# One transpose of raw queries taken off TensorE, and four small interruptions of a projection joined into two

## The reference

```python
h = rms_norm(x, pre_norm_w)
proj = h @ w_in                         # 4096 x 15408, columns: qa, za, ga, kc, vc, ksl, vsl, kw, vw, qb, kb, vb, zb
gates = sigmoid(ga + b_gate)            # 3 gates for each of 16 heads
kc, vc = compress(kc, ...), compress(vc, ...)     # gelu(blocks @ w1) @ w2: 15 compressed keys and values for each kv head
sc = q_raw @ kc.T                       # raw (not rotated) queries against compressed keys
p_cmp = softmax(where(valid, sc, NEG))
q_rot = rope(q, pos)                    # rotated queries, for the selected and the window branch
o = gates0 * (p_cmp @ vc) + gates1 * o_slc + gates2 * o_win
mix = concat([o * silu(za), ob * silu(zb)])
out = x + rms_norm(mix @ w_out, post_norm_w)
```

## Time and profile before

| what | value |
|---|---|
| median of 3 runs | 1765.64 us (1765.54 to 1766.12) |
| profiled execution: its own time | 1765.85 us |
| profiled execution: span | 1763.9 us |
| TensorE busy | 1757.8 us (100% of the span), 7902 matmuls |
| VectorE busy | 1153.4 us (65%) |
| ScalarE busy | 886.8 us (50%) |
| GpSimd busy | 598.9 us (34%) |
| granted TensorE clock | full in all 40 slices |
| bytes moved by DMA | 344.77 MB, mean 195 GB/s |

### The profile page before, as it was taken

The page is one execution under the profiler, slowest core; times in us unless marked ns, Lnnn a source line. Parts: engine busy times, 40 slices in busy tenths (PEclk is TensorE's granted clock), DMA queues, the critical chain, the costliest instruction groups (busy, mean ns, idle before and its releaser), DMA issues.

```text
span 1763.9 us, 22877 instructions
## 1 busy us (share of the span) xinstructions
PE 1757.8 (100%) x7902; PEld 1456.4 (83%) x7902; DVE 1153.4 (65%) x1192; ACT 886.8 (50%) x1216; POOL 598.9 (34%) x834
## 2 busy tenths in 40 slices
PE   9999999999999999999999999999999999999998
PEld 7888888888888888888888888888888888888886
DVE  7657656787888878656665666566655784444445
ACT  7643455464554545456435643564456554444443
POOL 3335303367593948721353034304431510000000
PEclk9999999999999999999999999999999999999999
DMA  9866687656565656666666666666666656667665
GB/s 294 254 199 188 188 248 229 179 161 185 157 189 151 185 160 174 183 197 182 179 195 196 182 181 197 194 190 176 191 194 191 190 185 217 213 213 212 213 202 204
DMA packets 184267, 344.77 MB, mean 195 GB/s; under 512 B 15216, under 2 KB 19568, under 8 KB 184176
## 3 DMA queue, kind: packets, MB, share of 16 engines
q1 hardware_dynamic: 183456, 342.58, 66.2%
q10 hardware_dynamic: 720, 0.93, 0.1%
HBM read 339.27 MB, written 4.19 MB: 195 GB/s over the span
## 4 chain that ended last, share of the span: by engine, by line
PE 99%; DMA 0%; ACT 0%; SPq 0%; DVE 0%; ACTq 0%; issue 0%
PE acc L640 31%; PE acc L646 31%; PE acc L643 31%; PE acc L821 1%; PE scores L810 0%; PE scores L709 0%; DMA raw<-in_w_in 0%; PE scores L742 0%; PE scores L741 0%; PE scores L740 0%; PE heads L757 0%; PE heads L758 0%; PE heads L759 0%; PE scores L665 0%; PE heads L692 0%; PE trans L657 0%
## 5 line engine op out<-in xcount | busy, mean ns | idle before, releaser
L1239 DVE TENSOR_TENSOR w_parts<-raw,w_parts 128x1024 fp32r<-128x1024 f32 x620 | 784.4, 1266 | 556.9 <-ACT w_parts L929 555.3
L929 ACT ACTIVATE w_parts<-raw 128x1024 fp32r<-128x1024 f32 x620 | 656.2, 1059 | 662.6 <-PE acc L646 649.6
L640 PE MATMUL acc<-w_parts,x_parts 128*128 128x512 f32 x2424 | 946.7, 391 | 0.2 <-DVE w_parts L1239 0.2
L646 PE MATMUL acc<-w_parts,x_parts 128*128 128x512 f32 x2424 | 943.8, 389 | 0.0
L643 PE MATMUL acc<-w_parts,x_parts 128*128 128x512 f32 x2424 | 943.3, 389 | 0.0
L646 PEld LDWEIGHTS acc<-w_parts,x_parts 128*128 128x128 f32 x2424 | 455.1, 188 | 95.8 <-DVE x_parts L1281 0.3
L640 PEld LDWEIGHTS acc<-w_parts,x_parts 128*128 128x128 f32 x2424 | 455.3, 188 | 93.4 <-issue 0.6
L643 PEld LDWEIGHTS acc<-w_parts,x_parts 128*128 128x128 f32 x2424 | 455.3, 188 | 93.0
L515 POOL COPY rot<-tok_b 32x256 f32<-32x256 f32 x120 | 86.9, 724 | 140.6 <-DVE tok_b L1613 135.7
L499 POOL TENSOR_TENSOR rot<-tok_a,trig 128x512 f32<-128x512 f32 x18 | 30.6, 1699 | 260.5 <-ACT tok_a L935 121.4
L515 POOL COPY b_first_t<-probs 32x128 f32<-32x128 f32 x64 | 31.1, 485 | 163.1 <-DVE probs L1686 160.6
(11 more groups left out here) (240 smaller groups left out, 1010.1 us busy)
## 6 DMA issues: line engine op xcount, KB each, us to landing
raw<-in_w_in SPq DMA_DIRECT2D x478, 512.0 KB, 3.7
raw<-in_w_out SPq DMA_DIRECT2D x128, 512.0 KB, 4.3
raw<-in_w SPq DMA_DIRECT2D x16, 512.0 KB, 4.7
x_tok<-in_x SPq DMA_DIRECT2D x16, 256.0 KB, 5.3
xt_raw<-in_x_t SPq DMA_DIRECT2D x7, 512.0 KB, 6.2
wpost<-in_post_w SPq DMA_DIRECT2D x8, 256.0 KB, 5.1
out<-y SPq DMA_DIRECT2D x3, 512.0 KB, 2.8
out<-y SPq DMA_DIRECT2D x5, 256.0 KB, 2.1
```

Of the source, the lines that this page charges most:

```text
L640: nc.tensor.matmul(o, stat_hi, mov_hi, start=(k == 0), stop=False)
L646: last = nc.tensor.matmul(o, stat_lo, mov_hi, start=False, stop=(k == KB - 1))
L929: nc.scalar.activation(w_hi[:, n % SPLIT_SLOTS, :, 0:width], raw[:, n % RAW_SLOTS, :, 0:width], ACT.Copy).then_inc(hi_ready, 1)
L1239: V.tensor_tensor(w_lo[:, s, :, 0:width], raw[:, n % RAW_SLOTS, :, 0:width], w_hi[:, s, :, 0:width].bitcast(F32), ALU.subtract).then_inc(l ...
```

## The change

Tile 1 of each group's raw queries is turned by VectorE (one transpose of 32x32 blocks of 128x512, in place in `tok_a`, at `at` 0, ahead of the split of pair 3), and the 16 blocks are moved to `qraw_t` by GpSimd (rows 0 and 1 of blocks: eight copies of 32x128) and by ScalarE (row 2 at `at` 1 and row 3 at `at` 2: four copies each, the first four ahead of `take_fill` of tile 0). TensorE's second `transpose4` and ScalarE's second `take_fill` go. TensorE waits for both movers ahead of pair 3. GpSimd does its copies ahead of the rotation of tile 0. In chunk `C_QA0` the gates' products follow the hidden layer's ahead of pair 2, and the compressed keys' stand with the values' ahead of pair 9; gates and keys are written to the bank `scores` in place of `trans`. ScalarE takes the keys at `at` 9 in place of 7.

```diff
@@ -70,7 +70,7 @@
 FILL_TRIG, FILL_HIDDEN, FILL_GATE, FILL_KC, FILL_VC, FILL_A = 0, 1, 2, 3, 4, 5
-FILLS_A = 2
+FILLS_A = 1
 TILES_ROTATED = 4
@@ -313,6 +313,9 @@
         heads_taken = sem("heads_taken")
+        q_turned = sem("q_turned")
+        q_moved_pool = sem("q_moved_pool")
+        q_moved_act = sem("q_moved_act")
         q_cos_ready = sem("q_cos_ready")
@@ -538,15 +541,24 @@
             nc.gpsimd.memset(pc_t[:, :, :, :, :].bitcast(F32), 0.0).then_inc(pc_zeroed, 1)
+            pool.wait_ge(pc_zeroed, 1)
             pool.wait_ge(tr_free, FILL_TRIG + 1)
             def rotate_a(g):
+                pool.wait_ge(q_turned, g + 1)
+                move_blocks(tok_a[:, 1:2, :].rearrange("p t (h d) -> p t h d", h=HPG),
+                            qraw_t[:, :, P:SEQ].rearrange("p h (t q) -> p t h q", t=1),
+                            range(QUARTERS * QUARTERS // 2)).then_inc(q_moved_pool, 1)
+                pool.wait_ge(q_moved_pool, g + 1)
                 for t in range(TILES):
...
                     cos = turn_t[:, 1, cols].unsqueeze(1).broadcast_to([P, HPG, P])
-                    pool.wait_ge(tr_free, FILL_A + t + 1 + FILLS_A * g)
+                    if t == 0:
+                        pool.wait_ge(tr_free, FILL_A + 1 + FILLS_A * g)
+                    else:
+                        pool.wait_ge(q_moved_act, g + 1)
                     nc.gpsimd.tensor_tensor(turned, qraw_t[:, :, cols], cos, ALU.mult).then_inc(q_cos_ready, 1)
@@ -696,12 +708,13 @@
-                if n in (1, 2):
-                    t = n - 1
-                    pe.wait_ge(acc0_free if t == 0 else acc1_free, c)
-                    transpose4(tok_a[:, t, :], fill + t)
+                if n == 1:
+                    pe.wait_ge(acc0_free, c)
+                    transpose4(tok_a[:, 0, :], fill)
                 if n == 3:
-                    pe.wait_ge(tr_free, fill + 2)
+                    pe.wait_ge(tr_free, fill + 1)
+                    pe.wait_ge(q_moved_pool, g + 1)
+                    pe.wait_ge(q_moved_act, g + 1)
@@ -835,27 +848,23 @@
                     last.then_inc(tr_done, 1)
-                if n == 3:
                     pe.wait_ge(gate_moved, 2)
-                    pe.wait_ge(tr_free, FILL_GATE)
                     for t in range(TILES):
                         for j in range(2):
-                            last = nc.tensor.matmul(trans[:, t * N_GATE:(t + 1) * N_GATE],
+                            last = nc.tensor.matmul(scores[:, t * N_GATE:(t + 1) * N_GATE],
                                                     gate_sum[:, t * P:(t + 1) * P],
...
                     last.then_inc(tr_done, 1)
-                if n == 7:
+                if n == 9:
                     pe.wait_ge(gelu_ready, 1)
...
                     for j in range(2):
-                        last = nc.tensor.matmul(trans[:, 0:64], w2_sb[:, 0, j, :], gelu[:, j * P:j * P + 64],
+                        last = nc.tensor.matmul(scores[:, 0:64], w2_sb[:, 0, j, :], gelu[:, j * P:j * P + 64],
                                                 start=(j == 0), stop=(j == 1))
                     last.then_inc(tr_done, 1)
-                if n == 9:
                     pe.wait_ge(rows_ready, 1)
-                    pe.wait_ge(tr_free, FILL_VC)
                     for g in range(GROUPS):
@@ -1028,8 +1037,8 @@
                                          ).then_inc(tanh_done, 1)
-                if at == 7:
-                    take_fill(FILL_KC, kc_t[:, :], trans[:, 0:64], 0.5)
+                if at == 9:
+                    take_fill(FILL_KC, kc_t[:, :], scores[:, 0:64], 0.5)
                 if at == 12:
@@ -1057,18 +1066,25 @@
-            def move_quarters(src, dst, rows, cols):
+            def move_quarters(src, dst, rows, cols, t=slice(0, TILES)):
                 rows, cols = slice(rows * QUARTER, (rows + 1) * QUARTER), slice(cols * QUARTER, (cols + 1) * QUARTER)
-                return nc.scalar.activation(dst[cols, :, :].rearrange("p h (t q) -> p t h q", t=TILES)[:, :, :, rows],
-                                            src[rows, :, :].rearrange("p t (h d) -> p t h d", h=HPG)[:, :, :, cols],
+                return nc.scalar.activation(dst[cols, :, :].rearrange("p h (t q) -> p t h q", t=TILES)[:, t, :, rows],
+                                            src[rows, :, :].rearrange("p t (h d) -> p t h d", h=HPG)[:, t, :, cols],
                                             ACT.Copy)
...
                     if at in (1, 2):
-                        take_fill(fill + at - 1, qraw_t[:, :, (at - 1) * P:at * P])
+                        if at == 1:
+                            act.wait_ge(q_turned, g + 1)
+                        for cols in range(QUARTERS):
+                            last = move_quarters(tok_a, qraw_t, at + 1, cols, slice(1, 2))
+                        if at == 1:
+                            take_fill(fill, qraw_t[:, :, 0:P])
+                        else:
+                            last.then_inc(q_moved_act, 1)
                     if at in (4, 5):
@@ -1419,7 +1435,7 @@
                         last = V.scalar_tensor_tensor(gates[:, t, :, :].rearrange("p h b -> p (h b)"),
-                                                      trans[:, t * N_GATE:(t + 1) * N_GATE], r[t], b_gate,
+                                                      scores[:, t * N_GATE:(t + 1) * N_GATE], r[t], b_gate,
                                                       ALU.mult, ALU.add)
@@ -1504,8 +1520,11 @@
             def crossed_halves(t, g, fill):
-                dve.wait_ge(tr_free, fill + t + 1)
-                if t == 1:
+                if t == 0:
+                    dve.wait_ge(tr_free, fill + 1)
+                else:
+                    dve.wait_ge(q_moved_pool, g + 1)
+                    dve.wait_ge(q_moved_act, g + 1)
                     dve.wait_ge(q_rot_ready, 1 + 2 * g)
@@ -1522,6 +1541,9 @@
                     at = n - LEAD
+                    if at == 0:
+                        dve.wait_ge(acc1_free, c)
+                        V.transpose(tok_a[:, 1, :], tok_a[:, 1, :]).then_inc(q_turned, 1)
                     if at in (2, 3):
```

## The result

The changed kernel takes 1770.43 us (median of 11 runs, 1770.12 to 1770.70) against 1765.97 us (11 runs, 1765.54 to 1766.62): ratio 1.0024, 95% interval 1.0016 to 1.0033. It is slower by 4.46 us, 0.25%, where 2 us less were forecast, and lies outside the forecast range of 1762.8 to 1767.0. The profiled execution has a span of 1768.3 us.

What follows compares the result with a forecast made beforehand. TensorE alone was taken to bound the kernel. Its terms, 1.96 + 0.08 = 2.04 us less, gave 1763.6 us against a median of 1765.64, called "same"; range 1762.8 to 1767.0.

Steps and rivals of the forecast that it cites:

- What bounds the kernel: Whole run: TensorE alone carries the chain, its longest wait 1.2 us, so nothing another engine does costs time now.
- The gain: TensorE, four groups: one interruption with four transposes fewer in each, 0.49 us apiece, 1.96 us less.
- the joining: TensorE's small products of gates and compressed keys: two interruptions fewer at 0.04 us each save 0.08 us.
- rival 2: Interruptions on TensorE cost more, so joining saves up to 0.98 us: 2.94 us less, 1762.7 us; chance 0.05.
- TensorE's new wait: Scores with compressed keys, 446.37 in group 1, wait for ScalarE's and GpSimd's copies; 0.4 to 1.9 us spare, no wait.
- Behind it ... Cost 0: After GpSimd's copies: tile 0's cosine product up to 2 us later, 2.5 us spare at pair 6, cost 0.
- The absorption: VectorE's second sine product stood behind the split of pair 5 anyway (448.2), which absorbs most of the delay.
- VectorE's part: Added transpose, 0.70 us a group, ahead of the split of pair 3, hidden by 1.84 us of idle time: cost 0.
- ScalarE's part: Block copies at 0.32 us move the fill of tile 0 and the split of pair 4 by 0.3 us: cost 0.
- Rival 1: Wait ahead of pair 3: GpSimd starved of the port; +1.6 us, chance 0.14, or about +8 us, chance 0.06.
- the starved case: Ahead of pair 3, GpSimd's copies blocked 6.4 us: 2.4 us a group, net +7.6, 1773.2 us; chance 0.06.
- waits further back: Unplaced later waits, counted "as much again" as the starved case within the 0.08 for over 3.5 us slower.

Runs made afterwards that it cites:

- e3: Changed kernel, but GpSimd makes one 128x256 copy in place of eight of 32x128, so half of tile 1's raw queries are not in place: 1767.03 us.
- e12: Kernel before, but each ScalarE fill (128x512) is done in eight pieces of 128x64: 1767.29 us, ratio 1.0007.
- e4: Changed kernel, but VectorE masks the first unit of scores ahead of the split of pair 8; nothing left out: 1769.34 us, ratio 1.0019.
- e9: Changed kernel, but VectorE writes tile 1's sine product into tile 0's half of `tok_a` and no longer waits for tile 0's rotation: 1769.43 us, ratio 1.0020.

## Why the prediction was wrong, point by point

- **What bounds the kernel.** TensorE had no wait, that was right. "Nothing that another engine does costs time now" was right too, but I read it as if there were room. A view of waits shows what is late; it does not show what is nearly late.
- **The gain.** 0.48 us for each of four transposes and 0.06 for the joining were there. Both terms of the sum stand; rival 2 is out.
- **TensorE's new wait.** GpSimd's copies ended at 445.12, ScalarE's at 444.94, TensorE came at 446.98. Counted from the chunk's start I had 6.8 to 8.3 us for GpSimd and it was 6.79. No wait, as forecast. A ScalarE copy of 32x128 took 0.31 us (I took 0.32), VectorE's transpose 0.71.
- **The step that failed is "Behind it ... Cost 0".** I had the cosine product of tile 0 up to 2 us late (it was 2.77), let that delay go down VectorE's queue only as far as the remainder of tile 0 (pair 6), found 2.5 us spare there, and stopped. Two things were wrong. The absorption: I said that the second sine product stood behind the split of pair 5 anyway, which would take up most of the delay. But I had not asked what the late cosine product would meet. It met the first sine product, ahead of that split: 2.40 us in place of 1.39. So the split itself started 0.95 us later, nothing was absorbed, and VectorE was 1.16 us late from there on. And the end of the walk: the same queue still held the mask that frees the bank for the second unit, with 0.31 us to spare before, less than the 0.49 that the gain itself takes off. e3 shows the two apart: without the eight copies 3.6 of the 5.5 us are gone, and the first group, where VectorE is on time, still loses 0.29. e12 shows the other half: with TensorE as before and VectorE 0.43 us late, 0.28.
- **VectorE's part and ScalarE's part, "Cost 0"**, were wrong by little: put at nothing, worth about 0.25 us in three of four groups (e3), through the fill of tile 0.
- **Rival 1** had the right cause, GpSimd and the port, and the right sign, but at the wrong door: its price was for the wait ahead of pair 3, which never came. Measured: 1.37 us a group instead of 0.9, ahead of pair 7; and when that wait is taken away (e4), part of it comes up at the third unit and at the first values.
- **The chances.** I gave slower by over 3.5 us 0.08. Of that 0.06 was the starved case, which left 0.02 for waits further back, where the loss came ("as much again" does not fit these figures). All my rivals had their waits at places that the change touches.
- **The last 0.8 us** had no term in the sum at all.

## What to carry to other kernels

When one engine has no wait at all, list its hand-overs with their spare before moving work off it: every microsecond taken from it shortens each spare behind, and in-order queues carry a delay on to all that stand behind, so follow a delayed step to the end of the stage, not to the next consumer. Work that is moved to a helper engine is charged there first to what the helper did already: here eight copies in front of a rotation, not the copies themselves. And ask what a late instruction will now collide with: the cosine product, 2.8 us late, ran beside a sine product and made it 1.0 us longer. A wait that a view shows need not be where the time was lost: the 1.18 us ahead of the second sine product only took the place of time that the split had lost before.

## What the hardware showed that I had not expected

Who gets the port between VectorE and GpSimd turned on 0.1 us. In the kernel before, GpSimd's addition

```profile
445.78 1.29 POOL L553 TENSOR_TENSOR rot<-rot,rot_tmp 128x512 f32<-128x512 f32 x1 [2.65 <-DVE rot_tmp L1513]
```

started 0.09 us ahead of the split of pair 5 at 445.87, and the split took 2.29 us; in the changed kernel the split started 0.12 us ahead, took 1.22, and the addition 2.26. For VectorE it made no difference: the second sine product ended 4.90 us behind the first either way. Taking a semaphore away between them (e9) gained only 0.25 us a group, as the product then took 3.36 us in place of 2.47. That a GpSimd instruction that reads SBUF and a VectorE instruction with two SBUF inputs exclude each other for a whole instruction is what the Trainium skill says in "SBUF — State Buffer", section "Who interferes with whom"; these durations agree. And the last output transfer's 0.8 us came and went with one 8 KB packet of instructions among its own, in ten of ten kernels and none of six. What puts that packet there, the added semaphores or the number of ScalarE's or GpSimd's instructions did not show.
